# Toeplitz column products beside a batch's transposes, first-layer rows requested one unit later, and positions loaded first in a two-layer state-space and attention trunk

## The reference

```python
for l in range(DEPTH):                       # 2 layers, 1024 tokens, width 1024
    mod = (silu(c) @ w_ada[l] + b_ada[l])    # six vectors of 1024: sh1, sc1, g1, sh2, sc2, g2
    h = rms_norm(x, norm1_g[l]) * (1 + sc1) + sh1
    z = h @ w_in[l]                          # u 512, cq 256, ckv 128, kr 32, gate_a 1024, gate_b 1024
    y_a = s5_mixer(u, ...) @ w_a_out[l]      # 32 groups, 64 complex states, scan over tokens
    y_b = mla_mixer(cq, ckv, kr, positions, cos, sin, ...) @ w_b_out[l]
    merged = sigmoid(gate_a) * y_a + sigmoid(gate_b) * y_b
    x = x + g1 * (merged @ w_out[l])
    h = rms_norm(x, norm2_g[l]) * (1 + sc2) + sh2
    x = x + g2 * ((silu(h @ w_gate[l]) * (h @ w_up[l])) @ w_down[l])
return rms_norm(x, final_g)
```

## Time and profile before

| what | value |
| --- | --- |
| median of 3 runs | 3113.15 us |
| profiled execution, whole time | 3116.92 us |
| profiled execution, span of the records | 3115.1 us |
| PE matmul busy | 3023.9 us (97%) |
| DVE busy | 1557.8 us (50%) |
| ACT busy | 1002.7 us (32%) |
| POOL busy | 865.8 us (28%) |
| mean granted TensorE clock | 0.988 |

### The profile page before, as it was taken

The page is one execution under the profiler, slowest core; times in us unless marked ns, Lnnn a source line. Parts: engine busy times, 40 slices in busy tenths (PEclk is TensorE's granted clock), DMA queues, the critical chain, the costliest instruction groups (busy, mean ns, idle before and its releaser), DMA issues.

```text
span 3115.1 us, 36606 instructions
## 1 busy us (share of the span) xinstructions
PE 3023.9 (97%) x14680; PEld 2547.0 (82%) x14680; DVE 1557.8 (50%) x1954; ACT 1002.7 (32%) x1412; POOL 865.8 (28%) x506
## 2 busy tenths in 40 slices
PE   6989999999999999999999999999999999999998
PEld 5877789988878888888878888998887888888886
DVE  7866577765143233232368995787534222232224
ACT  3423367761231111111143335777223111111112
POOL 0344222232322222222244552232232222222223
PEclk9999999999999999999999999999999999999999
DMA  7555410024221121221125661001441111111111
GB/s 272 166 155 166 129 41 12 25 68 149 101 82 61 61 75 61 61 67 49 48 102 161 187 185 55 16 25 38 135 135 41 48 54 48 48 48 48 48 52 71
DMA packets 279220, 264.26 MB, mean 85 GB/s; under 512 B 46737, under 2 KB 237329, under 8 KB 277650
## 3 DMA queue, kind: packets, MB, share of 16 engines
q1 hardware_dynamic: 252464, 217.66, 22.8%
q10 hardware_dynamic: 26594, 44.32, 3.9%
HBM read 218.59 MB, written 40.96 MB: 83 GB/s over the span
## 4 chain that ended last, share of the span: by engine, by line
PE 82%; DVE 8%; ACT 3%; DMA 2%; issue 2%; POOL 1%; ACTq 1%; SPq 0%; DVEq 0%; POOLq 0%
PE ps L552 23%; PE ps L554 22%; PE ps L555 22%; PE ps L1324 3%; PE ps L1344 2%; PE ps L1345 2%; PE ps L1310 2%; PE ps L1305 2%; PE ps L1309 2%; DMA raw<-in_w_in 1%; DVE t_ring L2066 1%; DVE h_lo L2076 1%; DVE z_tmp L2219 1%; PE ps L1171 1%; ACTq L1666 0%
## 5 line engine op out<-in xcount | busy, mean ns | idle before, releaser
L536 POOL TENSOR_TENSOR wlo<-raw,whi 128x1024 fp32r<-128x1024 f32 (+3 forms) x283 | 535.2, 1899 | 1916.6 <-ACT whi L528 1916.6
L528 ACT ACTIVATE whi<-raw 128x1024 fp32r<-128x1024 f32 (+3 forms) x290 | 242.8, 859 | 1504.3 <-PE ps L555 1374.7
L552 PE MATMUL ps<-h_hi,whi 128*128 128x512 f32 x2176 | 701.4, 396 | 17.5 <-DVE h_lo L2076 16.3
L554 PE MATMUL ps<-h_lo,whi 128*128 128x512 f32 x2176 | 693.2, 393 | 0.0
L555 PE MATMUL ps<-h_hi,wlo 128*128 128x512 f32 x2176 | 692.2, 392 | 0.0
L552 PEld LDWEIGHTS ps<-h_hi,whi 128*128 128x128 f32 x2176 | 409.8, 190 | 105.6 <-DVE h_lo L2076 20.2
L554 PEld LDWEIGHTS ps<-h_lo,whi 128*128 128x128 f32 x2176 | 413.2, 190 | 86.8
L555 PEld LDWEIGHTS ps<-h_hi,wlo 128*128 128x128 f32 x2176 | 412.5, 190 | 87.5
L2442 DVE TENSOR_TENSOR silu<-silu,ps 128x1024 f32<-128x1024 f32 x44 | 53.7, 1221 | 760.3 <-PE ps L555 758.2
L2460 DVE SCALAR_TENSOR_TENSOR x_sb<-ps,mod,x_sb 128x1024 f32<-128x1024 f32 x160 | 203.2, 1280 | 162.2 <-PE ps L555 162.2
L552 PE MATMUL ps<-hid_hi,whi 128*128 128x512 f32 x704 | 222.3, 390 | 0.0
(11 more groups left out here) (255 smaller groups left out, 4248.7 us busy)
## 6 DMA issues: line engine op xcount, KB each, us to landing
ada_raw<-in_w_ada SPq DMA_DIRECT2D x64, 512.0 KB, 4.4
raw<-in_w_in SPq DMA_DIRECT2D x92, 256.0 KB, 4.9
raw<-in_w_gate SPq DMA_DIRECT2D x88, 256.0 KB, 3.2
raw<-in_w_up SPq DMA_DIRECT2D x88, 256.0 KB, 3.2
raw<-in_w_down SPq DMA_DIRECT2D x88, 256.0 KB, 2.8
gate_scratch<-gst ACTq DMA_DIRECT2D x32, 512.0 KB, 3.9
gl<-gate_scratch SPq DMA_DIRECT2D x32, 512.0 KB, 4.3
ada_rows<-in_w_ada SPq DMA_DIRECT2D x16, 512.0 KB, 5.5
```

The costliest lines, as they stand in the source:

```text
L528: last = act.activation(dst(whi[:, s, :]), src(raw[:, s, :]), ACT.Copy)
L536: last = pool.tensor_tensor(dst(wlo[:, s, :]), src(raw[:, s, :]), dst(whi[:, s, :].bitcast(F32)), ALU.subtract)
L552: pe.matmul(o, w_h, x_h, start=first, stop=False)
L554: pe.matmul(o, w_h, x_l, start=False, stop=False)
```

## The change

Four things change, and no instruction is added or taken away.

1. PE: the Toeplitz column products of batch b move from behind the state matmuls (part 1) to behind the transposes (part 0), with their wait on `toe_col_done`.
2. DVE: the addition that makes `toe_col` moves from between the state multiplications and their sum to the head of `states(b)`, ahead of the wait for the state matmuls.
3. SP, stage of gates: the pair of rows at step t is t-3 in layer 1 as before, and t-4 in layer 0 (`behind = 1 + S5_LAG[l] // 2`).
4. Start: SP issues the positions first, then the rotary constants, both on a semaphore of their own (`angle_loaded`), then `first_c`, the columns and the query positions. DVE begins the angles on those two alone. It waits for the other three loads ahead of the query positions, and for the Silu ahead of the first row product.

```diff
--- before.py
+++ after.py
@@ -36,7 +36,7 @@
 ROUND = 12582912.0
 MAX_ANGLE = 3.1415925
 ROPE_ROWS = 6
-CONSTS = 5
+CONSTS = 3
 SSM_GROUP, SSM_STATE = 16, 64
 DVE_CONSTS = 6
 
@@ -360,6 +360,7 @@
         unit_used = count("unit_used", UNITS, credit=1)
         waited = count("waited", 0)
         const_loaded = count("const_loaded", 0)
+        angle_loaded = count("angle_loaded", 0)
         x_in_loaded = count("x_in_loaded", 0)
         pool_const = count("pool_const", 0)
         dve_const = count("dve_const", 0)
@@ -628,11 +629,12 @@
 
         @block.sync
         def _(sp):
-            for dst, src in ((cols[:, :, :], row_consts), (rope_sb[:, :], rope_const), (posq_i[:, :], pos_q)):
+            sp.dma_start(pos_i[:, :], positions[0].rearrange("(o n) -> o n", o=1).broadcast_to([P, SEQ]))\
+                .then_inc(angle_loaded.sem, 16)
+            sp.dma_start(rope_sb[:, :], rope_const).then_inc(angle_loaded.sem, 16)
+            sp.dma_start(first_c[:, :], c.broadcast_to([P, D])).then_inc(const_loaded.sem, 16)
+            for dst, src in ((cols[:, :, :], row_consts), (posq_i[:, :], pos_q)):
                 sp.dma_start(dst, src).then_inc(const_loaded.sem, 16)
-            sp.dma_start(first_c[:, :], c.broadcast_to([P, D])).then_inc(const_loaded.sem, 16)
-            sp.dma_start(pos_i[:, :], positions[0].rearrange("(o n) -> o n", o=1).broadcast_to([P, SEQ]))\
-                .then_inc(const_loaded.sem, 16)
 
             def load_ada(l, m, k, number, dst=ada_raw):
 
@@ -728,8 +730,9 @@
                         gate_unit(U_GATE + t, t)
                     else:
                         latent_unit(t - 2 * KT)
-                    if 3 <= t < 2 * KT + 3:
-                        ada_pair(t - 3)
+                    behind = 1 + S5_LAG[l] // 2
+                    if behind <= t < 2 * KT + behind:
+                        ada_pair(t - behind)
                     b, odd = divmod(t - 1 - S5_LAG[l] // 2, 2)
                     if t == 3:
                         ut_load(0)
@@ -1159,6 +1162,11 @@
                         last = pe.transpose(ps[:, 4, g * P:(g + 1) * P],
                                             be[:, b % 2, g, :, :].rearrange("p j m -> p (j m)"), ident[:, 0:P])
                     last.then_inc(s5_tr.sem, 1)
+                    wait(pe, toe_col_done, l, b)
+                    for g in range(4):
+                        last = pe.matmul(ps[:, 6, g * M:(g + 1) * M], be[:, b % 2, g, :, :].rearrange("p j m -> p (j m)"),
+                                         c_n[:, first_group(b) + g, :], start=True, stop=True)
+                    last.then_inc(toe_col_mm.sem, 1)
 
                 def batch_states(b):
 
@@ -1170,11 +1178,6 @@
                     for g in range(4):
                         last = pe.matmul(ps[:, 5, g * P:(g + 1) * P], mt[:, j, g, :], ut[:, j, g, :], start=True, stop=True)
                     last.then_inc(v_mm.sem, 1)
-                    wait(pe, toe_col_done, l, b)
-                    for g in range(4):
-                        last = pe.matmul(ps[:, 6, g * M:(g + 1) * M], be[:, j, g, :, :].rearrange("p j m -> p (j m)"),
-                                         c_n[:, first_group(b) + g, :], start=True, stop=True)
-                    last.then_inc(toe_col_mm.sem, 1)
 
                 def batch_outputs(b):
 
@@ -1968,10 +1971,9 @@
                 dve.tensor_tensor(mod[:, m, :], mod[:, m, :], bias, ALU.add).then_inc(mod_ready.sem, 1)
 
             dve.wait_ge(pool_const.sem, 2)
-            dve.wait_ge(act_const.sem, 1)
             dve.wait_ge(dve_const.sem, DVE_CONSTS)
 
-            dve.wait_ge(const_loaded.sem, 16 * CONSTS)
+            dve.wait_ge(angle_loaded.sem, 32)
             steps = [DVE_CONSTS]
 
             def link(inst):
@@ -2000,6 +2002,7 @@
             link(dve.tensor_scalar(pos_f[:, :], pos_i2[:, :], 65536.0, None, ALU.mult))
             link(dve.tensor_scalar(pos_i2[:, :], pos_i[:, :], 65535, None, ALU.bitwise_and))
             link(dve.tensor_copy(pos_lo[:, :], pos_i2[:, :]))
+            dve.wait_ge(const_loaded.sem, 16 * CONSTS)
             link(dve.tensor_scalar(posq_i2[:, :], posq_i[:, :], 16, None, ALU.arith_shift_right))
             link(dve.tensor_scalar(hi_bias[:, :], posq_i2[:, :], 65536.0, None, ALU.mult))
             link(dve.tensor_scalar(posq_i2[:, :], posq_i[:, :], 65535, None, ALU.bitwise_and))
@@ -2021,6 +2024,7 @@
                 link(dve.tensor_scalar(tk[:, :], ang_k[:, :], rope_sb[:, 4:5], None, ALU.mult))
                 link(dve.scalar_tensor_tensor(tk[:, :], sin_t[:, :], rope_sb[:, 5:6], tk[:, :], ALU.mult, ALU.add))
 
+            dve.wait_ge(act_const.sem, 1)
             for n in range(2 * KT):
                 k, m = divmod(n, 2)
                 dve.wait_ge(rows_loaded[n % 4].sem, 16 * (n // 4 + 1))
@@ -2203,17 +2207,17 @@
                         rot(dve.tensor_tensor(rot_b[:, side, :, :], t0, t1, op))
 
                 def states(b):
+                    wait(dve, toe_col_mm, l, b + 1)
+                    wait(dve, toe_loaded, l, 16 * CH * b)
+                    dve.tensor_tensor(toe_col[:, :, :].rearrange("p m g -> p g m"), d_col[:, first_group(b):first_group(b) + 4, :],
+                                      ps[:, 6, 0:4 * M].rearrange("p (g m) -> p g m", g=4), ALU.add)\
+                        .then_inc(toe_col_done.sem, 1)
                     wait(dve, v_mm, l, b + 1)
                     v = ps[:, 5, :].rearrange("p (g c) -> p g c", g=4)
                     low, high = slice(0, 64), slice(64, P)
                     rot(dve.tensor_tensor(t0, rot_b[:, 0, :, :], v, ALU.mult), False)
                     rot(dve.tensor_tensor(t1[low], rot_b[low, 1, :, :], v[high], ALU.mult), False)
                     rot(dve.tensor_tensor(t1[high], rot_b[high, 1, :, :], v[low], ALU.mult))
-                    wait(dve, toe_col_mm, l, b + 1)
-                    wait(dve, toe_loaded, l, 16 * CH * b)
-                    dve.tensor_tensor(toe_col[:, :, :].rearrange("p m g -> p g m"), d_col[:, first_group(b):first_group(b) + 4, :],
-                                      ps[:, 6, 0:4 * M].rearrange("p (g m) -> p g m", g=4), ALU.add)\
-                        .then_inc(toe_col_done.sem, 1)
                     rot(dve.tensor_tensor(t2, t0, t1, ALU.add))
                     for g in range(4):
                         rot(dve.tensor_tensor_scan(out=g_sb[:, g, :],
```

## The result

The changed kernel takes 3082.64 us (median of 4 runs, 3079.31 to 3084.93) against 3114.15 us (4 runs, 3112.9 to 3116.7): a ratio of 0.9897, 95% interval 0.988 to 0.9914, a gain of 31.5 us. I had forecast 3072.5 us, a gain of 40.6 us. The time is inside the range given (3068 to 3089) but outside the forecast's own range (3068 to 3077). The profiled execution took 3082.38 us with a span of 3080.6 us, 34.5 us less than the one of before.

The account below looks back on a forecast made before the run. PE was taken as the bound, 97% busy, with idle time and slow clock in layer 0 to win. Terms 36.2 + 1.4 + 3.0 = 40.6 us took 3113.15 to 3072.5 us; own range 3068 to 3077, range given 3068 to 3089.

Parts of the forecast that it names:

- the pairs: Layer 0, batches 0 to 7: pairs one unit later make its stretch like layer 1's, 36.2 us less.
- the queue's load: Rival: weights late because of the queue's load, not the order; only the start moves, 3110 us; chance 0.04.
- the `ut` rival: Layer 0: `ut` stays late behind a pair, three of seven intervals lose 15.5 us again, 3088 us; chance 0.08.
- no wait at line 1179: Sign: the prediction is wrong if PE still waits there in every second batch of layer 0.
- did not become the bound: Rival: POOL stops DVE for its whole length in layer 0, DVE becomes the bound, 3128 us; chance 0.03.
- the cover for this edit is PE's half unit, and I cost it at 0: Toeplitz products and addition moved: costed at 0, losing at most 0.27 us per batch if DVE were the bound.
- the tail: Third latent unit behind layer 0's batches: without the wait its low clock goes, 1.4 us less; bounds 0 and 1.4.
- the start: Positions first: first row product near 19.3 us, first `h` matmul near 52.9, 3.0 us less; bounds 0 and 5.1.
- The sum: Whole kernel: 36.2 + 1.4 + 3.0 = 40.6 us less, median 3072.5 us.

Follow-up runs that it names:

- e1: Kernel before with only the pairs of rows one step later in layer 0: 3080.47 us, ratio 0.9893.
- e5: Changed kernel with layer 1's row pairs asked for one step earlier: 3124.28 us (one run).
- e4: Changed kernel with the Toeplitz products and the addition at their old places: 3077.32 us, ratio 0.9885.
- e8: e4 with the five first loads in the old order, DVE still waiting for positions and rope table alone: 3078.05 us, ratio 0.9887.
- e9: Changed kernel with ACT issuing a batch's eight Toeplitz loads ahead of `whi` and the sigmoid: 3079.68 us, ratio 0.9886.
- e6: Changed kernel with the addition back at its old place on DVE, the Toeplitz products staying ahead: 3080.36 us, ratio 0.9888.
- e7: Changed kernel with the Toeplitz products back behind the state matmuls on PE, the addition staying at the head of the states: 3076.6 us, ratio 0.9877.
- e11: Changed kernel with each batch's four state products done twice into the same bank: 3097.22 us (one run).
- e10: e4 with the first row tile of `w_ada` issued ahead of x: 3076.75 us, ratio 0.9881.
- e2: Kernel before with the start alone changed (load order, `angle_loaded`, DVE's three moved waits): 3112.09 us, ratio 0.9992.
- e3: Kernel before with the Toeplitz products and addition alone moved: 3117.67 us, ratio 1.0011.

## Why the prediction was right or wrong

**Right: the pairs.** The bound, the mechanism and the size were right. Layer 1 of the same trace was the model for layer 0, and e1 gave 36.1 us for a term of 36.2. e5 shows the reverse in the other layer. SP's order, not the queue's load, made the weights late.

**The range was luck in part.** The measured 3082.6 us lies inside 3068 to 3089 only because the range was stretched to the `ut` rival, which did not come true. Nothing in the forecast accounts for the part between 3077 and 3082.6 us; the steps below do.

**Right: no rival came true.** State inputs behind a pair cost nothing (no wait at line 1179), and DVE, at 164.83 us of 184.56, did not become the bound.

**Wrong: the step "the cover for this edit is PE's half unit, and I cost it at 0".** I compared the edit with DVE and with the addition, and took 1.7 us as the margin by which `toe_g` beats PE. I bounded a loss only by DVE (0.27 us per batch). I never asked what stood between the release of ACT's chain and PE's need of its result. The products were 0.9 us of that. In the changed kernel PE waits 2.3 us at the outputs and the stretch is 3.0 us longer than in e4 (184.56 against 181.55); layer 1's is 0.8 us longer (182.01 against 181.21). The medians of the changed kernel and e4 differ by 5.3 us, of which the two stretches explain 3.8. The benefit that I saw in the addition's new place was not there either: with it at the old place PE waits for nothing in layer 0's stretch of e1 and e4. My margin of 1.7 us came from ACT's shortest path. Batch 0 needs no new activation table; batches 1 to 6 have a table load ahead of the sigmoid, and the eight loads take up to 6.2 us to issue instead of 5.15. ACT in batch 1 of the changed kernel:

```profile
173.77 1.28 ACT L1692 ACT_TABLE_LOAD   x1
...
176.49 6.18 ACTq L1651 DMA_DIRECT2D toe<-toe_col  x8
```

The table load alone makes 1.7 us into 0.4, less than the 0.9 us taken away. In layer 1, where the loads of batches 1 to 6 took 5.2 to 5.6 us, PE waited once. Why they issue faster there was not tried.

**Wrong: the tail.** The step that failed is "The low clock follows the wait and the small matmuls of batch 7. Without the wait I take 1.4 us". That wait, in the trace before, was this one:

```profile
365.65 1.16 PE L1171 MATMUL ps<-ut,mt 128*128 128x128 f32 x8 [1.77 <-ACT mt L1547]
```

It is gone, and in the changed kernel the third latent unit still takes 12.61 us at a clock of 0.86, like the earlier trace rows. A new wait of 0.58 us stands ahead of it, but the other traces do not make that the cause. The unit in the changed kernel, in e4, in e8 and in e9, in the columns of the earlier trace rows:

```profile
334.45:347.06 12.61, 12.61 (x48) 10.23 (x49) 8.91 (x16) 5.92 (x11) 6.41 (x6) 0.86 0.03 7
331.57:342.60 11.03, 11.03 (x50) 8.91 (x49) 8.41 (x17) 5.78 (x11) 3.60 (x6) 1.00 0.07 15
329.84:342.45 12.61, 12.61 (x50) 10.23 (x50) 8.40 (x17) 5.90 (x11) 3.60 (x6) 0.86 0.06 12
331.60:342.60 11.00, 11.00 (x49) 9.09 (x50) 8.59 (x16) 5.91 (x11) 5.35 (x6) 1.00 0.15 48
```

e8 has no wait and the low clock, e9 has the wait and the full clock. Of the six kernels with the wait (the changed one, e5, e6, e7, e9, e11) four show 0.86 to 0.88 there and two 1.00; of the four with early weights and without it (e1, e4, e8, e10) two show 0.86 or 0.87 and two 1.00. e4 and e8 have the same PE order. So the 1.4 us were there in some executions and not in others, and what decides is not known.

The wait itself is for DVE's three multiplies of batch 7: the last ends at 334.35, and PE goes on at 334.45. The products used to cover them. In e7 they lie behind the states again, but there the addition waits for them and holds the multiplies back, and PE waits 0.62 us.

**Wrong in size: the start.** Term 3.0 us, measured 1.6 us at the first `h` matmul and 2.2 us in e2's median. The step that failed is "its row, issued at 7.49, took 11.8 us and lands at 19.3". With the positions first SP took 5.00 us to issue x instead of 4.38 and came to the rows at 8.11, and the row took 12.0 us and let DVE go on at 20.32. The same five loads stand ahead of it in both orders, so it is their order and not their bytes: in the four kernels with the old order (before, e1, e3, e8) SP comes to the rows at 7.45 to 7.63, in the eight others that issue x first at 7.79 to 8.36. Why SP issues x more slowly then was not tried. In those eight the first product starts anywhere from 19.5 to 20.8 us, so part of the shortfall of a single trace is chance.

**The sum.** The profiled difference lacks 6.1 us to 40.6. In the trace 3.4 are in layer 0's stretch, 1.3 in the start (the state matmuls of batch 0 came 1.7 us earlier, not 3.0), 1.1 in the tail (from batch 7's state matmuls to the end of the third latent unit 0.3 us were gained, not 1.4) and 0.8 in layer 1's stretch; the stages between and behind give 0.5 back. The other 3 us lie between that difference (34.5) and that of the medians (31.5).

## What to carry to other kernels

Where one stretch of a program does the same work faster than another, compare their issue orders row by row; the difference can be taken as a term almost whole. Before an instruction is moved at "no cost", ask of the engine it runs on: which other engine's chain is released before its old place and needed behind it, and by how much does that chain win in its longest batch, not in its first? An engine that is always busy pays for work once, but that work is also another chain's time. And before loads are reordered, free the waiting engine from a semaphore that it does not need: here that gave the whole gain of the start, and the new order of the loads only made SP come later to the rows.

## What the runs showed of the hardware

The same DVE instructions of a stretch took from 140 us (e5, layer 1, 192 instructions) over 141.19 and 164.83 to 174.60 us (e9, 191 instructions), in kernels that give it the same work in another order. e9 has a bare example. DVE and POOL at the same time:

```profile
258.19 1.23 DVE L1961 CUSTOM_DVE_ANT_0 ada_raw<-ada_raw,c_bc 128x1024 f32<-128x1024 f32 x1 [0.21 <-DVE h_st L2237]
...
259.34 3.42 DVE L1961 CUSTOM_DVE_ANT_0 ada_raw<-ada_raw,c_bc 128x1024 f32<-128x1024 f32 x1
```

```profile
258.33 3.35 POOL L537 TENSOR_TENSOR wlo<-raw,whi 128x1024 fp32r<-128x1024 f32 x1 [10.82 <-ACT whi L529]
```

The same product takes 1.23 us and then 3.42 us; it ends at 262.76, 1.1 us behind POOL's end at 261.68. By the lock that the Trainium skill describes (SBUF — State Buffer, section SBUF: two separate sides) DVE would stand still until POOL is through, and this row agrees. So does the product before it: it had begun 0.14 us ahead of POOL and took its usual 1.23 us.

The small loads of the start landed later once a 512 KB load stood ahead of them: `cols`, 87 KB, took 1.9 us from issue to landing before and 5.3 us in the changed kernel (2.0 us in e8). With both 512 KB loads behind the small ones (e8), the Silu's table load began at 6.24 instead of 8.74 us.
